# Layer norm statistics from VectorE's statistics instruction, in a two-layer encoder trunk

## What is computed

```python
def layer_norm(x, g, b):
    mu = jnp.mean(x, axis=-1, keepdims=True)
    xc = x - mu
    var = jnp.mean(xc * xc, axis=-1, keepdims=True)
    return xc * lax.rsqrt(var + LN_EPS) * g + b

for l in range(DEPTH):                                   # DEPTH = 2
    x = layer_norm(ALPHA * x + 0.5 * swiglu(x, ffn1...), ln1_g[l], ln1_b[l])
    h = x @ w_in[l]          # q, k, v of 8 stick-breaking heads and 8 chunked softmax heads
    mixed = concat(head_rmsnorm(stick_breaking(...)), head_rmsnorm(chunk_attention(...)))
    x = layer_norm(ALPHA * x + mixed @ w_out[l], ln2_g[l], ln2_b[l])
    x = layer_norm(ALPHA * x + 0.5 * swiglu(x, ffn2...), ln3_g[l], ln3_b[l])
```

## Time and profile before

| | us |
|---|---|
| median of 3 runs | 976.34 |
| the profiled execution, device time | 977.56 |
| its span, first to last instruction | 975.8 |
| TensorE (PE) busy | 963.2 (99%) |
| TensorE weight loads (PEld) busy | 884.1 (91%) |
| VectorE (DVE) busy | 809.4 (83%) |
| ScalarE (ACT) busy | 562.9 (58%) |
| GpSimd (POOL) busy | 21.2 (2%) |
| mean granted TensorE clock | 0.998 of full |

### The profile page before, as it was taken

One profiled execution on the slowest core, in us unless ns is written; L12 is line 12 of the kernel. 1 busy time (PEld: TensorE's weight loads), 2 busy tenths in 40 slices (PEclk: granted clock), 3 DMA queues, 4 the chain that ended last, 5 costly groups with the idle time before them and its releaser, 6 DMA issues.

```text
span 975.8 us, 16987 instructions
## 1 busy us (share of the span) xinstructions
PE 963.2 (99%) x6570; PEld 884.1 (91%) x6570; DVE 809.4 (83%) x892; ACT 562.9 (58%) x623; POOL 21.2 (2%) x53
## 2 busy tenths in 40 slices
PE   9999999999999999999999999999999999999996
PEld 9899999899778999999899999998987789999996
DVE  5998887855898998887889988878558889988885
ACT  5755554558884655554566555545688656555543
POOL 1000000001000000000000000000010000000000
PEclk9999999999999999999999999999999999999999
DMA  8766654662343656454626574544642536655444
GB/s 302 256 222 253 218 172 171 215 240 106 131 163 139 216 192 237 173 211 174 219 98 211 209 301 172 216 173 173 216 147 99 180 136 216 241 173 212 171 170 153
DMA packets 34651, 187.27 MB, mean 192 GB/s; under 512 B 3888, under 2 KB 3888, under 8 KB 19504
## 3 DMA queue, kind: packets, MB, share of 16 engines
q1 hardware_dynamic: 33120, 177.22, 51.0%
q0 software_dynamic: 1488, 9.45, 2.5%
HBM read 185.61 MB, written 1.05 MB: 191 GB/s over the span
## 4 chain that ended last, share of the span: by engine, by line
PE 84%; DVE 10%; ACT 3%; issue 2%; DMA 1%; POOL 0%; SPq 0%; DVEq 0%; POOLq 0%; ACTq 0%
PE bank L1225 25%; PE bank L1226 25%; PE bank L1227 25%; PE bank L1366 7%; DVE w_lo L809 3%; ACT w_hi L458 2%; PE bank L1288 1%; DMA raw<-stream 1%; DVE soft_t L1103 1%; DMA kT<-first 1%; DVE mx L1106 1%; DVE stick_t L1085 1%; POOL stick_t L417 0%; DVE soft_t L1119 0%; DVE soft_t L1123 0%
## 5 line engine op out<-in xcount | busy, mean ns | idle before, releaser
L1225 PE MATMUL bank<-xT_hi,w_hi 128*128 128x256 f32 x1456 | 412.2, 283 | 0.0
L1227 PE MATMUL bank<-xT_hi,w_lo 128*128 128x256 f32 x1456 | 412.0, 283 | 0.0
L1226 PE MATMUL bank<-xT_lo,w_hi 128*128 128x256 f32 x1456 | 412.0, 283 | 0.0
L458 ACT ACTIVATE w_hi<-raw 128x2048 fp32r<-128x2048 f32 x120 | 229.1, 1912 | 132.9 <-PE bank L1227 127.4
L1225 PEld LDWEIGHTS bank<-xT_hi,w_hi 128*128 128x128 f32 x1456 | 279.1, 192 | 3.7 <-issue 0.7
L1226 PEld LDWEIGHTS bank<-xT_lo,w_hi 128*128 128x128 f32 x1456 | 279.2, 192 | 3.0
L1227 PEld LDWEIGHTS bank<-xT_hi,w_lo 128*128 128x128 f32 x1456 | 279.1, 192 | 0.0
L803 DVE TENSOR_TENSOR w_lo<-raw,w_hi 128x2048 fp32r<-128x2048 f32 x87 | 199.2, 2290 | 45.1 <-ACT w_hi L458 44.8
L1225 PE MATMUL bank<-w_hi,h_hi 128*128 128x512 f32 x284 | 111.8, 394 | 1.5 <-DVE soft_t L972 1.1
L1226 PE MATMUL bank<-w_lo,h_hi 128*128 128x512 f32 x284 | 111.4, 392 | 0.0
L1227 PE MATMUL bank<-w_hi,h_lo 128*128 128x512 f32 x284 | 110.5, 389 | 0.0
(11 more groups left out here) (166 smaller groups left out, 1233.8 us busy)
## 6 DMA issues: line engine op xcount, KB each, us to landing
raw<-stream SPq DMA_DIRECT2D x110, 1024.0 KB, 4.9
raw<-stream SPq DMA_DIRECT2D x112, 512.0 KB, 4.6
lnp<-ln_gb POOLq DMA_DIRECT2D x6, 1024.0 KB, 5.6
band<-rel_band POOLq DMA_DIRECT2D x2, 1024.0 KB, 9.1
qT<-first SPq DMA_DIRECT2D x2, 512.0 KB, 4.0
kT<-first SPq DMA_DIRECT2D x2, 512.0 KB, 6.6
xn<-x POOLq DMA_DIRECT2D x1, 1024.0 KB, 5.3
out<-xn SPq DMA_DIRECT2D x4, 256.0 KB, 2.0
```

The lines of the kernel that those rows point to most:

```text
L458: nc.scalar.activation(w_hi[:, at(slot if into is None else into)], raw[:, slot, :], ACT.Copy).then_inc(hi_ready, 1)
L1225: nc.tensor.matmul(o, w[0], x[0], start=start, stop=False, skip_group_check=again)
L1226: nc.tensor.matmul(o, w[0], x[1], start=False, stop=False, skip_group_check=again)
L1227: return nc.tensor.matmul(o, w[1], x[0], start=False, stop=stop, skip_group_check=again)
```

## The change

The two accumulated sums of line 896, the mean of line 903 and ScalarE's square of line 503 go. Behind each residual addition VectorE reads the half just written with its statistics instruction (`bn_stats`, 512 elements per partition in, 6 numbers out), behind a wait for that addition; a second instruction (`bn_aggr`) turns the 12 numbers of a block into mean and variance. ScalarE's logarithm reads the variance directly. Steps per block on the `ln_step` semaphore go from 8 to 10. The semaphore `var_done` goes. Everything else in the program is as before.

```diff
-                act.wait_ge(ln_step, n * LN_STEPS + LN_MEAN)
-                nc.scalar.activation(flat(scratch), xn[:, tb, :], ACT.Square, bias=sums[:, tb, 2:3],
-                                     accum_out=sums[:, tb, 3:4]).then_inc(var_done, 1)
-                act.wait_ge(var_done, n + 1)
-                nc.scalar.activation(lt[:, tb, 0:1], sums[:, tb, 3:4], ACT.Ln, scale=1.0 / D,
+                act.wait_ge(ln_step, n * LN_STEPS + LN_STATS)
+                nc.scalar.activation(lt[:, tb, 0:1], moments[:, tb, 1:2], ACT.Ln,
                                      bias=eps[:, 0:1]).then_inc(lnv_done, 1)
...
-                                                            op0=ALU.mult, op1=ALU.add,
-                                                            accum_out=sums[:, tb, half:half + 1]))
+                                                            op0=ALU.mult, op1=ALU.add))
+                        after(k[0])
+                        done(nc.vector.bn_stats(stats[:, tb, 6 * half:6 * half + 6], xn[:, tb, cols]))
                     after(k[0])
-                    minus_mean = sums[:, tb, 2:3]
-                    done(nc.vector.tensor_scalar(minus_mean, sums[:, tb, 0:1], sums[:, tb, 1:2], -1.0 / D,
-                                                 ALU.add, ALU.mult))
-                    assert k[0] == LN_MEAN
+                    done(nc.vector.bn_aggr(moments[:, tb, :], stats[:, tb, :]))
+                    assert k[0] == LN_STATS
                     after(k[0])
...
-                                                            scalar=minus_mean, in1=lnp[:, 0, cols],
-                                                            op0=ALU.add, op1=ALU.mult))
+                                                            scalar=moments[:, tb, 0:1], in1=lnp[:, 0, cols],
+                                                            op0=ALU.subtract, op1=ALU.mult))
...
-                    dve.wait_ge(var_done, n + 1)
-                    done(nc.vector.tensor_scalar(lt[:, tb, 2:3], sums[:, tb, 3:4], -0.5 / D, -0.5 * LN_EPS,
+                    done(nc.vector.tensor_scalar(lt[:, tb, 2:3], moments[:, tb, 1:2], -0.5, -0.5 * LN_EPS,
                                                  ALU.mult, ALU.add))
```

More of the change, by code:

```diff
@@ L83, in unit_slots @@
     return order, before, seen
-LN_MEAN, LN_STEPS = 3, 8
+LN_STATS, LN_STEPS = 5, 10
 SLOT, FILLED, PER_LAYER = unit_slots()
@@ L186, in trunk @@
         eps = sb("eps", [P, 2])
-        sums = sb("sums", [P, 2, 4])
+        stats = sb("stats", [P, 2, 12])
+        moments = sb("moments", [P, 2, 2])
         lt = sb("lt", [P, 2, 5])
@@ L248, in trunk @@
         ln_step = sem("ln_step")
-        var_done = sem("var_done")
         lnv_done = sem("lnv_done")
```

## The result

The changed kernel takes 984.25 us, the median of 5 runs (984.14 to 985.94), against 976.34 for the one before (5 runs): ratio 1.0082, 95% interval 1.0071 to 1.0092, so 7.9 us slower, 6.9 to 9.0. The forecast was 984.6, the range 980.5 to 988.0.

A forecast was written before the change was run, and what follows sets the result against it. TensorE, busy 963.2 of 975.8 us, was taken as the bound. Delays of 3 x 1.50 + 2 x 1.19 + 1.37 = 8.25 us on the median 976.34 gave 984.6 us, range 980.5 to 988.0.

The forecast's parts named there:

- TensorE bounds, and ScalarE's saving is worth nothing by itself: Whole kernel: TensorE busy 963.2 of 975.8 us; only making it wait, and the tail after its last product, counts.
- ScalarE's wait of 0.40 us in block 0 goes: Before line 922 in block 0: VectorE's 0.40 us wait for ScalarE's square pass disappears, so line 930 is less late.
- The statistics instruction takes 0.69 us, by the reduction's row: VectorE: 0.69 us for 512 elements, taken from line 1106's reduction at 686 ns.
- Two elements at a time: Rival: VectorE's statistics instruction takes 0.42 us, so the loss is 2.4 us, 978.8; chance 0.08.
- two passes: Rival: VectorE's statistics instruction takes 1.22 us, so the loss is 21 us, 997.3; chance 0.04.
- The price that goes by outputs: Rival: statistics instruction on VectorE costs like a small one, no measurable loss: +0.5 us, 976.9; chance 0.03.
- Block 0's gap of 0.39 us can't hold it: Between block 0's additions, first layer norm: statistics needs 0.72 us, gap is 0.39, so the second addition starts 0.33 late.
- Block 1's centring is late by 1.62 and 1.39: VectorE's centring of block 1: 1.62 us late in the first layer norm, 1.39 in the second.
- Slack of 0.12 and 0.20: TensorE's weight loads for the second `x_lo`: 0.12 us spare in layer norms one, three, four; 0.20 in two, five.
- What follows hangs on TensorE, so the delay counts in full: After inner layer norms: TensorE's lateness counts in full, 1.50 us in first, third, fourth, 1.19 in second, fifth.
- the rival of cover in attention: After layer norms one and four, TensorE's idle time in attention gives back 1.6 us: +6.6, 982.9; chance 0.08.
- The last layer norm, 1.37: Last layer norm: block 1 wins back its 0.40 us wait, and the stores start 1.37 us late.

The follow-up runs named there:

- idle_square: The change plus twelve ScalarE square passes of 1024 elements over constants, behind the exponential, result unused; 985.44 us.
- scalar_variance: The change with the variance taken again from a ScalarE square pass, without subtracting the mean; the mean still from the statistics instructions; 987.21 us.
- late_stats: The change with both statistics instructions of a block moved behind its two additions; 986.82 us.
- extra_stats: The change with one more statistics instruction per block 1, result unused, ahead of the aggregation (24 become 30); 988.17 us.
- last_only: The kernel before with the statistics instruction only in the last of six layer norms, the five inner ones unchanged; 978.39 us beside 976.81.
- block0_only: The kernel before with the statistics instruction for token block 0 of every layer norm, block 1 the old way; 978.73 us beside 976.81.

## Why the prediction was right, step by step

- *TensorE bounds, and ScalarE's saving is worth nothing by itself:* shown by idle_square. *ScalarE's wait of 0.40 us in block 0 goes:* shown by the change's own row (186.24 to 186.43, no wait) and by scalar_variance, which gets 0.3 of it back; the other 0.09 is the shorter form of the square there.
- *The statistics instruction takes 0.69 us, by the reduction's row:* 0.694. Two elements at a time and two passes fall with it, and with 284, 418 and 694 ns for 128, 256 and 512 elements neither is left in any form. The price that goes by outputs, 0.21 for a small instruction, falls too. The Trainium skill's 58 cycles plus one per element at 0.96 GHz ("VectorE: DVE Perf Modes", "The TRN2 errata") gives an estimate of 0.59 us; the slope, 1.04 ns for each element, agrees with these runs, the fixed part of 0.06 us doesn't: they show 0.15. The prediction had taken only that line of the section. The section itself says that this line comes out too short for a single instruction and that the measured fixed part is about 150 cycles, which gives an estimate of 0.69 us here and agrees with 0.694.
- *Block 0's gap of 0.39 us can't hold it:* shown by the additions, 1.32 us apart, and from the other side by late_stats, which gives the gap up and loses 2 us. Block 0's centring is 1.02 us late and its scaling 0.63 in the first layer norm, where 1.08 and 0.68 were forecast.
- *Block 1's centring is late by 1.62 and 1.39:* it was 1.51 in the first, and 1.29 in the second (307.75 - 298.33 = 9.42 us behind the layer norm's first addition, where it was 306.55 - 298.42 = 8.13). The term that was mis-sized is the aggregation, twice 0.04 too dear.
- *Slack of 0.12 and 0.20:* this step failed. It is 0.00 and 0.10, because the lead of a weight load over its matmul was read from the transposes (0.23) and not from the pair that waits for `x_lo` (0.02). The error of 0.1 has the other sign than the aggregation's, and so the forecast per layer norm, 1.50 and 1.19, met 1.53 and 1.19: agreement to a few hundredths is luck. The range doesn't hang on it, since with both put right the steps give 1.54 and 1.21, and the sum is 8.33.
- *What follows hangs on TensorE, so the delay counts in full:* extra_stats shows it, 0.52 to 0.56 and once 0.48 for a centring that is 0.52 later, and the rival of cover in attention falls. The fourth distance is 0.05 to 0.08 above the first and third in the change. last_only, whose fourth layer norm is as before, has 0.04 there and 0.02 and 0.01 in the others, so part of it lies in the trace of before that all are compared with; why the rest, stays open.
- *The last layer norm, 1.37:* 1.28, of it 0.08 again the aggregation. last_only shows that it stands alone.
- Putting the sum on the median was right: the sum of the distances is 8.28 us and the medians differ by 7.9, within the interval.

## What to carry to other kernels

Work that moves from an idle engine to one whose results the bound engine waits for costs all of its latency that finds no idle time there, and what it freed on the idle engine was worth nothing here; ask of each such place what idle time the new instruction can fall into, and count it instruction by instruction. A new instruction is best put where its engine waits anyway: the same two statistics instructions cost 2 us less around the wait between the additions than behind it. Where runs scatter by as much as an effect, compare the distances between two fixed instructions in the traces: here they repeat within some 0.05 us.

## What was not expected of the hardware

- The traces here, of kernels that are alike up to the first layer norm, already differ before it (181.91 to 184.60 us from the start of the span to its first addition) and hardly after it where the kernels are alike. What differs there was not looked into.
- A square over 1024 elements on ScalarE took 1154 ns with a per-partition bias and 1062 without (1.06 in the row of scalar_variance), and 1047 over a broadcast constant, without bias and without accumulated sum.
- Transposes that came late on TensorE gave some of the delay back: in block0_only the scaled half is about 0.63 us late and the distance grows by 0.44. Before, the load of block 0's first transpose started at 188.80 and its matmul at 189.03; in block0_only both start at 189.51. Counted from the first addition the load is 0.61 late and the matmul 0.38, so what was given back is the lead of 0.23. Late products of the second `x_lo`, whose load had no such lead, gave nothing back in the first, third and fourth layer norms.
